# Merge-gate logits by seven half-size products in a two-layer decoder kernel; head 0's final state after the last retention step

## The chip, the cores and the metric

One NeuronCore of a Trainium2 chip runs the whole step as one launch. The metric is the device time in microseconds (us), lower is better. The program is in float32 throughout. The engines are TensorE (PE; its weight loads are listed apart as PEld), VectorE (DVE), ScalarE (ACT), GpSimd (POOL) and SyncE (SP, which issues the weight loads by DMA).

## The reference, cut to what matters

Two trunk layers of a hybrid decoder over 288 tokens: 256 of a prompt and 32 of a sample group (8 sequences of 4). Of each layer only the token-mixing half matters here:

```python
z = h @ p["w_in"][l]
u, v, q, k, vr, gr, ga, gb = jnp.split(z, ...)          # ga and gb: 1024 columns each
a = chunk_spatial_gating(gelu(u), layernorm(gelu(v)), w_s, b_s)
y, r_new = retention(rotary(q), rotary(k), vr, r0, chunk)   # 4 heads; r_new is an output
b = jax.nn.silu(gr) * head_groupnorm(y)
merged = sigmoid(ga) * (a @ w_a_out) + sigmoid(gb) * (b @ w_b_out)
x = x + gt1 * (merged @ w_o)
```

After it comes a mixture of 32 experts (16 pairs), which the change doesn't touch. `r_new` for the prompt is, for each head, one (256 x 512) matrix: the "final state" below.

## The kernel before, in words

**Weights** come from HBM as slots of 2 MB, [128, 4096] in float32, in the order in which the steps use them, into a ring of four buffers. SyncE issues the load of slot n when the last product on slot n-4 is done (`LAST_TILE`), or, where that buffer held a retention state that is written back, when the store has landed. `LOADS` gives the order.

**The order of the work** is written out by hand in `layer_steps`. Every engine walks the same list of steps and does its own part of each, in order; semaphores tie them together. PSUM has eight banks; seven of them are handed to the tiles of the steps in turn (`use`, `turn % 7`), so a tile has the bank of the tile seven places before it, and `wait_free` (L573) makes PE wait until that one has been read.

**Two ways to a product.** A direct slot (`feature_major`) multiplies 1024 inputs by 512 outputs for all 288 tokens: 4 column tiles of 8 matmuls with 288 columns. A slot by seven products (`feature_seven` for features on partitions, `token_seven` for tokens on partitions) is one Strassen-Winograd step: weights and tokens are cut in halves, and seven half-size products m1, m3, c11, m5, m6, m7, m4 take the place of eight; for features each is 2 column tiles of 4 matmuls with 144 columns. It needs four sums of the tokens (`token_sums`: s1, s3, s2, s4, made once and used by every slot with that input), four differences of weight blocks on DVE (`turn_first` L1627; `turn_rest` L1635, L1637, L1639; each 128 x 1024 elements, in place in the ring) and six additions that put the results together on DVE (`join`, L1650 to L1660). m1, m3 and c11 need no changed weights; m3 needs s4; m5, m6, m7 and m4 each wait for one more weight difference. ACT copies m1 out (`first_partial`) and applies the activation to the four quarters as they come (`bend`).

Before the change u, v (second slot), ga, a, q, k, vr, gr and b are made by seven products, and gb and the output projection o directly. gb has two slots: slot 0 is one step, ("gb", 0), and slot 1 is split into two steps of two column tiles each, ("gb", 1) and ("gc", 1).

**The stretch around the change** (layer 0 is at 280 to 428 us of the span, layer 1 runs the same steps some 774 us later):
- ("gr", 0..3), the swish-gate slots, alternate with ("st", 0..3), the sample states: PE makes eight outer products of a state, DVE adds them into the ring buffer (L2033, eight updates a state), ACT stores it back ("store").
- Then ("r1", 0), ("gb", 0), ("st", 4), ("y", 0), ("f", 0), ("fout", 0), and for the heads 1 to 3: keys transposed ("kt"), scores ("sc"), the next state ("st"), the output of the first and second chunk ("r1", "y"). For each r1 and y, DVE takes the moments (L1536, L1538) and subtracts the mean and multiplies by the gate (L2025); POOL makes the inverse root (L706, L708); ACT multiplies by it and raises `b_ready`.
- ("f", i) is the final state of head i, four matmuls into two banks; ("fout", i) copies these on ACT into a buffer and stores it. The heads in `LATE_FINAL` have theirs later, beside the router, and head 0 not.
- ("ysum", 0): the same normalisation for the samples. ("bts", 0) and ("bt", 0..7): the gated result is transposed; ACT takes bts and the even bt out of PSUM, DVE the odd ones. PE waits ahead of bts until all nine parts are normalised (`b_ready`). During ("gc", 1) DVE makes the token sums of the transposed result (`token_sums(bT, sums_b)`, L1612 to L1617), and ("b", 0..3) follow.

sgb, the sigmoid of gb, lies in the buffer `ovd`. That buffer holds the token sums for `token_seven` (`sums_t`) until the last gr slot has used them.

Of the kernel before, what the change touches and what calls it, by code (L numbers as in the profile page):

```python
# [9 lines left out]
D = 1024  # L10
# [38 lines left out]
LATE_FINAL = [(1, 2, 3), (1, 2, 3)]  # L49


def layer_steps(l):
# [14 lines left out]
    for n, step in enumerate(columns):  # L67
# [38 lines left out]
SEVEN_KINDS = ("u", "ga", "a", "q", "k", "vr", "gr")  # L106
# [9 lines left out]
BENT_AT = {s: n for n, s in enumerate((l, s) for l in range(DEPTH) for s in STEPS[l] if seven(s) and s[0] in ("v", "u", "ga", "gr"))}  # L116


def tiles_of(step, l):
# [5 lines left out]
    if step == ("gb", 1):  # L125
        return ["c0", "c1"]
    if kind == "gc":
        return ["c2", "c3"]
    if kind in ("gb", "o"):
        return ["c0", "c1", "c2", "c3"]  # L130
# [77 lines left out]
for _l in range(DEPTH):  # L208
    for _s in STEPS[_l]:
# [7 lines left out]
        elif _s in SLOT_OF and (_l, _s) not in LOADS:  # L217
            LOADS.append((_l, _s))
            if kind != "st":
                LAST_TILE[_l, _s] = (_l, ("gc", 1), "c3") if _s == ("gb", 1) else (_l, _s, tiles_of(_s, _l)[-1])  # L220
# [32 lines left out]
for _name, _width in [  # L253
    ("ident", P), ("modfold", ROWS), ("eps", 1),
    ("tri", P), ("tri_incl", P), ("tri_copies", P), ("fold", P), ("cos", TOK), ("sin", TOK),
    ("decay", 2 * HEADS * P), ("xis", 2 * HEADS * NS), ("masks", P), ("mixmask", NS),
    ("zeta", HEADS), ("zeta0", HEADS), ("zetas", NB), ("iota", PACK), ("iota4", 4), ("iota8", 8), ("iota32", NE),
# [6 lines left out]
CFIRST = P + ROWS + 1  # L264
# [17 lines left out]
def constants():  # L282
# [10 lines left out]
    put("modfold", (p[:, None] % NS == np.arange(ROWS)[None, :]))  # L293
# [26 lines left out]
    put("iota", np.broadcast_to(np.arange(PACK), (P, PACK)))  # L320
# [30 lines left out]
def build(nc, stream, consts, params, x_in, c_in, gfin, y_out, state_out, state_sample_out, v_out):  # L351
    f32, i32 = mybir.dt.float32, mybir.dt.int32
    ALU, ACT, AX = mybir.AluOpType, mybir.ActivationFunctionType, mybir.AxisListType
    with ExitStack() as ctx:
# [3 lines left out]
        def sem(name):  # L358
            return ctx.enter_context(nc.semaphore(name))
# [10 lines left out]
        modp = sb("modp", [P, 2, 512])  # L370
        ones = sb("ones", [P, P])
# [49 lines left out]
        sgb = cut(ovd[:, :], KT, TOK)  # L421
# [7 lines left out]
        kz_late = cut(prm[:, ln_at:ln_at + D], 2, 2, DK)  # L429

# [5 lines left out]
        sums_h = sums_of(work[:, SG_AT + KT * TOK:SG_AT + 2 * KT * TOK], KT // 2, RIDE)  # L436
# [1826 lines left out]
```

## Time and profile before

| | us |
|---|---|
| median of three runs | 1594.88 (1594.32 to 1595.27) |
| the profiled execution, its own time | 1594.71 |
| its span in the trace | 1592.4 |
| PE busy (share of the span) | 1554.4 (98%) |
| DVE busy | 877.7 (55%) |
| ACT busy | 270.1 (17%) |
| POOL busy | 62.8 (4%) |
| chain that ended last: PE, issue, DMA, DVE, POOL, ACT | 84%, 8%, 4%, 1%, 1%, 1% |

The time of an execution is 2.3 us more than the span of its trace. Busy is the time in which an engine has an instruction in work. Matmuls are pipelined and their ends are modelled, so a matmul's own duration is longer than the distance to the next one; costs of PE are best read as differences between starts in the timeline. One float32 matmul of the program stands as two records in the trace.

### The profile page before, as it was taken

How to read it: one execution, taken by the hardware profiler on the slowest of the kernel's cores; microseconds unless marked ns; L12 is line 12 of the kernel's file. 1: busy time of each engine (PE TensorE's matmuls, PEld its weight loads, DVE VectorE, ACT ScalarE, POOL GpSimd, SP SyncE). 2: the span in 40 equal slices, each digit the busy share in tenths (PEclk: the TensorE clock that was granted, in tenths of full speed). 3: DMA queues.
4: the chain of work that ended last, by engine and by line, in shares of the span. 5: the costliest groups of instructions: out<-in, count | busy, mean ns of one | idle time of the engine just before them, and what ended most of it. 6: DMA issues, size and time to landing. Idle time of an engine off the chain costs nothing.

```text
span 1592.4 us, 24838 instructions
## 1 busy us (share of the span) xinstructions
PE 1554.4 (98%) x9958; PEld 1070.9 (67%) x9958; DVE 877.7 (55%) x1814; ACT 270.1 (17%) x556; POOL 62.8 (4%) x107
## 2 busy tenths in 40 slices
PE   7999999999999999999999999999999998999997
PEld 3999887775797544444459998877659965444443
DVE  2776864665662634434558777556476444433436
ACT  3110000112201421111131100011130032111111
POOL 0000000001001200000000000000010011000000
PEclk9999999999999999999999999999999999999999
DMA  9824666688843799999983355548895339999993
GB/s 396 331 110 159 266 264 233 269 343 327 322 159 126 302 411 421 421 421 421 423 341 141 128 204 229 203 151 323 320 363 210 131 130 355 421 421 421 421 421 130
DMA packets 49810, 461.41 MB, mean 290 GB/s; under 512 B 5968, under 2 KB 6224, under 8 KB 10144
## 3 DMA queue, kind: packets, MB, share of 16 engines
q1 hardware_dynamic: 44656, 414.38, 65.4%
q10 hardware_dynamic: 3456, 37.75, 5.7%
q0 software_dynamic: 1584, 7.69, 1.3%
q8 instruction: 81, 1.33, 0.3%
q14 instruction: 33, 0.27, 0.0%
HBM read 415.88 MB, written 43.91 MB: 289 GB/s over the span
## 4 chain that ended last, share of the span: by engine, by line
PE 84%; issue 8%; DMA 4%; DVE 1%; POOL 1%; ACT 1%; SPq 0%; DVEq 0%; POOLq 0%; ACTq 0%
PE ps L799 84%; DMA ring<-stream 1%; DMA ovd<-sorted_rows 1%; DMA sorted_rows<-work,packed_rows 1%; POOL sorted_rows L760 0%; ACT work L1263 0%; DMA cst<-consts 0%; POOL kzm L740 0%; POOL rstd L708 0%; DVE rope L1585 0%; SPq L674 0%; DVE hT L2148 0%; POOLq L707 0%; DVEq L1529 0%; ACT hT L1263 0%
## 5 line engine op out<-in xcount | busy, mean ns | idle before, releaser
L799 PE MATMUL ps<-work,ring 128*128 128x144 f32 (+1 forms) x2624 | 358.1, 298 | 0.0
L799 PEld LDWEIGHTS ps<-work,ring 128*128 128x128 f32 x2624 | 341.0, 190 | 13.6
L799 PE MATMUL ps<-ring,work 128*64 128x512 f32 x1536 | 339.2, 595 | 2.9 <-ACT work L1263 1.3
L799 PEld LDWEIGHTS ps<-ring,work 128*64 128x64 f32 x1536 | 113.3, 137 | 211.1 <-issue 210.4
L1263 ACT ACTIVATE work<-ps 128x256 f32<-128x256 f32 (+5 forms) x228 | 97.1, 434 | 748.4 <-PE ps L799 707.5
L799 PE MATMUL ps<-ring,hT 128*32 128x128 f32 (+2 forms) x1776 | 169.9, 312 | 3.0 <-ACT hT L1263 3.0
L799 PE MATMUL ps<-hT,ring 128*128 128x144 f32 (+1 forms) x1024 | 165.6, 317 | 0.0
L799 PEld LDWEIGHTS ps<-hT,ring 128*128 128x128 f32 x1024 | 145.8, 190 | 16.6 <-issue 3.6
L799 PE MATMUL ps<-work 128*128 128x288 f32 (+3 forms) x608 | 152.1, 393 | 3.4 <-DVE hT L2122 2.6
L799 PEld LDWEIGHTS ps<-ring,hT 128*32 128x32 f32 (+1 forms) x1776 | 126.1, 132 | 39.4 <-issue 26.5
L799 PEld LDWEIGHTS ps<-work 128*128 128x128 f32 (+1 forms) x608 | 100.7, 185 | 53.9 <-issue 26.9
L799 PE MATMUL ps<-ring,ovd 128*128 128x256 f32 x576 | 130.2, 379 | 0.0
L2092 DVE TENSOR_TENSOR work<-work,ps 128x256 f32<-128x256 f32 x32 | 13.5, 421 | 208.1 <-ACT work L1263 208.1
L799 PEld LDWEIGHTS ps<-ring,ovd 128*128 128x128 f32 x576 | 109.4, 190 | 14.9
L1697 DVE TENSOR_TENSOR hT<-hT,ps 128x288 f32<-128x288 f32 x224 | 99.1, 453 | 10.8 <-PE ps L799 7.0
L2033 DVE SCALAR_TENSOR_TENSOR ring<-ring,ps 128x512 f32<-128x512 f32 x128 | 78.1, 682 | 45.3 <-PE ps L799 45.3
L1635 DVE TENSOR_TENSOR ring<-ring 128x1024 f32<-128x1024 f32 x46 | 56.4, 1225 | 58.3 <-PE ps L799 57.4
L1263 ACT ACTIVATE work<-work 128x512 f32 (+4 forms) x122 | 58.9, 525 | 150.9 <-DVE work L1657 118.7
L1627 DVE TENSOR_TENSOR ring<-ring 128x1024 f32<-128x1024 f32 x46 | 56.2, 1222 | 28.3 <-PE ps L799 27.0
L1637 DVE TENSOR_TENSOR ring<-ring 128x1024 f32<-128x1024 f32 x46 | 56.4, 1225 | 4.2
L1639 DVE TENSOR_TENSOR ring<-ring 128x1024 f32<-128x1024 f32 x46 | 56.1, 1219 | 0.0
L2128 DVE COPY work<-ps 128x512 f32<-128x512 f32 x32 | 22.1, 692 | 54.9 <-PE ps L799 54.9
(221 smaller groups left out, 1105.6 us busy)
## 6 DMA issues: line engine op xcount, KB each, us to landing
ring<-stream SPq DMA_DIRECT2D x194, 1024.0 KB, 11.0
ring<-stream SPq DMA_DIRECT2D x95, 2048.0 KB, 8.8
state_sample_out<-ring ACTq DMA_DIRECT2D x16, 2048.0 KB, 7.6
state_out<-prm ACTq DMA_DIRECT2D x8, 512.0 KB, 4.3
work<-sorted_rows SPq DMA_DIRECT2D x6, 512.0 KB, 5.3
prm<-params SPq DMA_DIRECT2D x1, 2608.5 KB, 27.3
prm<-params POOLq DMA_DIRECT2D x1, 2608.5 KB, 16.8
cst<-consts SPq DMA_DIRECT2D x1, 1651.0 KB, 20.5
```

Source lines behind the costliest of these rows:

```text
L799: return nc.tensor.matmul(out, lhsT, rhs, start=start, stop=stop, **k)
L1263: return act.activation(out, in_, func, **k)
L1627: dve.tensor_tensor(b12, b12, b11, ALU.subtract).then_inc(weights_ready, 1)
L1635: dve.tensor_tensor(b22, b22, b12, ALU.subtract).then_inc(weights_ready, 1)
L1637: dve.tensor_tensor(b11, b22, b11, ALU.subtract).then_inc(weights_ready, 1)
L1639: dve.tensor_tensor(b21, b21, b22, ALU.subtract).then_inc(weights_ready, 1)
L1697: taken(dve.tensor_tensor(hT[:, ft, :], hT[:, ft, :], out[:, 0:TOK], ALU.add), key)
L2033: taken(dve.scalar_tensor_tensor(state[:, h, dt, :], state[:, h, dt, :], math.exp(decay(h) * NT), out[:, :], ALU.mult, ALU.add), key)
L2092: taken(dve.tensor_tensor(hid[:, :, :], hid[:, :, :], up, ALU.mult), (l, pair, "gu"))
L2128: taken(dve.tensor_copy(yslot[:, 512:1024], out[:, :]), (l, pair, "y1"))
```

## The change

Both gb slots are made by `feature_seven`, in one step each. The four token sums that they need, of hT in 144-token halves, no longer exist by then (their place has been used again), so POOL makes them once more in `ovd` when the last gr slot's product m7 is done. The second gb slot moves whole to behind the transposes, and head 0's final state moves from behind ("y", 0) to ahead of the transposes. bts moves behind the bt, and each bt waits only for its own part. Since the sums fill `ovd`, the gate values move: half of them to `modp` and a new buffer `gates`, the other half to `ovd` once the sums there are used. DVE makes the token sums of bT inside ("gb", 1), between the first weight difference and the other three. A constant that nothing read (`modfold`) goes and `iota` is cut from 576 to 64 columns.

```diff
-LATE_FINAL = [(1, 2, 3), (1, 2, 3)]
+LATE_FINAL = [(0, 1, 2, 3), (0, 1, 2, 3)]
...
-        + [("r1", 0), ("store", 3), ("gb", 0), ("st", 4), ("y", 0), ("store", 4), ("f", 0), ("fout", 0), ("kt", 1), ("sc", 1), ("st", 5), ("r1", 1), ("store", 5), ("y", 1)]
-        + [("kt", 2), ("sc", 2), ("st", 6), ("r1", 2), ("store", 6), ("y", 2), ("kt", 3), ("sc", 3), ("st", 7), ("r1", 3), ("store", 7), ("y", 3)] + ([] if 3 in LATE_FINAL[l] else [("f", 3), ("fout", 3)])
-        + [("ysum", 0), ("gb", 1), ("bts", 0)] + [("bt", i) for i in range(8)]
-        + [("gc", 1)] + [("b", i) for i in range(4)]
+        + [("r1", 0), ("store", 3), ("gb", 0), ("st", 4), ("y", 0), ("store", 4), ("kt", 1), ("sc", 1), ("st", 5), ("r1", 1), ("store", 5), ("y", 1)]
+        + [("kt", 2), ("sc", 2), ("st", 6), ("r1", 2), ("store", 6), ("y", 2), ("kt", 3), ("sc", 3), ("st", 7), ("r1", 3), ("store", 7), ("y", 3)]
+        + [("ysum", 0), ("f", 0), ("fout", 0)] + [("bt", i) for i in range(8)] + [("bts", 0), ("gb", 1)] + [("b", i) for i in range(4)]
...
-SEVEN_KINDS = ("u", "ga", "a", "q", "k", "vr", "gr")
+SEVEN_KINDS = ("u", "ga", "gb", "a", "q", "k", "vr", "gr")
...
-    ("ident", P), ("modfold", ROWS), ("eps", 1),
+    ("ident", P), ("eps", 1),
...
-    ("zeta", HEADS), ("zeta0", HEADS), ("zetas", NB), ("iota", PACK), ...
+    ("zeta", HEADS), ("zeta0", HEADS), ("zetas", NB), ("iota", CAP), ...
...
+        gates = sb("gates", [P, 2, TOK])
...
-        sgb = cut(ovd[:, :], KT, TOK)
+        modp_flat = modp.rearrange("p a w -> p (a w)")
+        sgb = [cut(modp_flat[:, 0:2 * TOK], 2, TOK), gates, cut(ovd[:, 2 * TOK:4 * TOK], 2, TOK), cut(ovd[:, 0:2 * TOK], 2, TOK)]
...
+        sums_g = sums_of(ovd[:, :], KT // 2, RIDE)
...
+            if kind == "gb":
+                return [cut(rope_flat[:, 0:2 * RIDE], 2, RIDE), cut(rope_flat[:, 2 * RIDE:4 * RIDE], 2, RIDE), cut(modp_flat[:, 2 * TOK:3 * TOK], 2, RIDE)]
...
+                    elif step == ("gr", 3):
+                        s1, s4, s2, s3 = sums_g
+                        half = KT // 2
+                        a11, a12, a21, a22 = hT[:, 0:half, RIGHT], hT[:, half:KT, RIGHT], hT[:, 0:half, LEFT], hT[:, half:KT, LEFT]
+                        wait_made(pool, (l, step, "m7"))
+                        pool.tensor_tensor(s1, a21, a22, ALU.add)
+                        pool.tensor_tensor(s3, a11, a21, ALU.subtract)
+                        pool.drain()
+                        pool.tensor_tensor(s2, s1, a11, ALU.subtract)
+                        pool.drain()
+                        pool.tensor_tensor(s4, a12, s2, ALU.subtract).then_inc(gate_sums_ready, 1)
...
                 product("m1", act[:, 0:half, RIGHT], 0, 0)
-                pe.wait_ge(sums_ready, 4 * l + sums_n)
+                if step[0] == "gb":
+                    pe.wait_ge(gate_sums_ready, l + 1)
+                else:
+                    pe.wait_ge(sums_ready, 4 * l + sums_n)
                 product("m3", s4, 1, 1)
...
-                        feature_major(l, step, hT, range(4) if i == 0 else range(2))
-                    elif kind == "gc":
-                        feature_major(l, step, hT, range(2, 4))
+                        feature_seven(l, step, hT, sums_g, 0)
...
                     elif kind == "bt":
+                        tt, q = i // 4, i % 4
+                        pe.wait_ge(b_ready, l * B_DONE + 2 * q + tt + 1)
                         out = wait_free(pe, (l, step, "t"))
...
-                    elif kind == "ga":
+                    elif kind in ("ga", "gb"):
                         first_partial(l, step)
                         bend(l, step, parts_of(step), ACT.Sigmoid)
-                    elif kind in ("gb", "gc"):
-                        for name in tiles_of(step, l):
-                            out = wait_made(act, (l, step, name))
-                            taken(apply(sgb[:, 4 * i + int(name[1]), :], out[:, 0:TOK], ACT.Sigmoid), (l, step, name))
...
-                    elif kind == "gc":
-                        wait_reads(dve, [(l, ("bts", 0), "t")] + [(l, ("bt", n), "t") for n in range(8)])
-                        token_sums(bT, sums_b)
+                    elif kind == "gb":
+                        turn_first(l, step)
+                        if i == 1:
+                            wait_reads(dve, [(l, ("bts", 0), "t")] + [(l, ("bt", n), "t") for n in range(8)])
+                            token_sums(bT, sums_b)
+                        turn_rest(l, step)
+                        join(l, step, *parts_of(step)[1:])
                     elif kind == "b":
...
                         if i == 0:
-                            wait_reads(dve, tiles(l, ("gb", 0), ("c0", "c1", "c2", "c3")) + tiles(l, ("gb", 1), ("c0", "c1")) + tiles(l, ("gc", 1), ("c2", "c3")))
+                            dve.wait_ge(bent, BENT_AT[l, ("gb", 1)] + 1)
```

## Rows read from the trace of the kernel before

**Rows 1.** The page: engines over the span, and the clock by slices.
```profile
PE 1554.4 (98%) x9958; PEld 1070.9 (67%) x9958; DVE 877.7 (55%) x1814; ACT 270.1 (17%) x556; POOL 62.8 (4%) x107
PEclk9999999999999999999999999999999999999999
```

**Rows 2.** Waits of PE over the span: total, times, longest.
```profile
PE ps L799 <- ACT work L1263: 10.9, 6, 8.6
...
PE ps L799 <- ACT prm L1263: 3.0, 4, 0.9
...
PE ps L799 <- DMA ring<-stream: 1.2, 2, 1.0
```

**Rows 3.** Timeline of PE, layer 0: start, us, form, count [idle before].
```profile
348.74 1.89 PE L799 MATMUL ps<-ring,hT 128*128 128x256 f32 x8
...
355.66 15.68 PE L799 MATMUL ps<-hT,ring 128*128 128x288 f32 x64
371.27 1.07 PE L799 MATMUL ps<-ring,prm 128*32 128x512 f32 x8
...
377.23 3.60 PE L799 MATMUL ps<-work,kz 128*128 128x512 f32 x8
380.66 0.60 PE L799 MATMUL ps<-cst,work 128*128 128x128 f32 x4
```

**Rows 4.** Timeline of PE, layer 0: start of the second q slot's seven products, and what follows them.
```profile
162.13 2.23 PE L799 MATMUL ps<-hT,ring 128*128 128x144 f32 x16
...
176.05 1.92 PE L799 MATMUL ps<-ring,cT 128*32 128x512 f32 x16
```

**Rows 5.** Timeline of DVE, layer 0, around the states 4 and 5.
```profile
358.81 0.75 DVE L2025 SCALAR_TENSOR_TENSOR work<-ps,moments,work 128x512 f32<-128x512 f32 x1
373.43 4.87 DVE L2033 SCALAR_TENSOR_TENSOR ring<-ring,ps 128x512 f32<-128x512 f32 x8 [13.87 <-PE ps L799]
...
379.52 0.75 DVE L2025 SCALAR_TENSOR_TENSOR work<-ps,moments,work 128x512 f32<-128x512 f32 x1
382.61 0.42 DVE L2012 TENSOR_TENSOR scT<-ps,cst 128x256 f32<-128x256 f32 x1 [2.34 <-PE ps L799]
...
384.66 4.87 DVE L2033 SCALAR_TENSOR_TENSOR ring<-ring,ps 128x512 f32<-128x512 f32 x8 [1.43 <-PE ps L799]
```

**Rows 6.** Weight differences on DVE (page, part 5: busy, mean ns).
```profile
L1635 DVE TENSOR_TENSOR ring<-ring 128x1024 f32<-128x1024 f32 x46 | 56.4, 1225 | 58.3 <-PE ps L799 57.4
```

**Rows 7.** Weight loads beside the 144-column products (page, part 5: busy, mean ns).
```profile
L799 PEld LDWEIGHTS ps<-work,ring 128*128 128x128 f32 x2624 | 341.0, 190 | 13.6
```

**Rows 8.** Line L755, additions on POOL: ns min/median/max, first and last start us.
```profile
L755 POOL TENSOR_TENSOR work<-work x12: 790/790/794, 492.0 to 1285.6; 128x288 f32<-128x288 f32 x12
```

**Rows 9.** Timeline of PE, layer 0, from the end of ("y", 3) to the first b slot.
```profile
408.26 7.92 PE L799 MATMUL ps<-hT,ring 128*128 128x288 f32 x32
416.02 4.09 PE L799 MATMUL ps<-cst,work 128*128 128x128 f32 x36
419.95 7.93 PE L799 MATMUL ps<-hT,ring 128*128 128x288 f32 x32
427.71 86.08 PE L799 MATMUL ps<-work,ring 128*128 128x144 f32 x576
```

**Rows 10.** Timeline of ACT, layer 0: fout, then the last scalings and bts, bt.
```profile
381.10 1.07 ACT L1263 ACTIVATE prm<-ps 128x512 f32<-128x512 f32 x2
...
412.25 0.72 ACT L1263 ACTIVATE work<-work,rstd 128x512 f32<-128x512 f32 x1 [1.24 <-POOL rstd L708]
414.22 0.72 ACT L1263 ACTIVATE work<-work,rstd 128x512 f32<-128x512 f32 x1 [1.25 <-DVE work L2040]
...
416.65 1.91 ACT L1263 ACTIVATE work<-ps 128x128 f32<-128x128 f32 x6
```

**Rows 11.** Timeline of DVE, layer 0: first token sum of bT, next weight difference.
```profile
421.00 1.36 DVE L1612 TENSOR_TENSOR work<-work 128x1152 f32<-128x1152 f32 x1 [0.16 <-DVE work L2045]
...
426.41 1.22 DVE L1627 TENSOR_TENSOR ring<-ring 128x1024 f32<-128x1024 f32 x1
```

More of the change, by code:

```diff
@@ L115 @@
 SEVEN_AT = {s: n for n, s in enumerate((l, s) for l in range(DEPTH) for s in STEPS[l] if seven(s))}
-BENT_AT = {s: n for n, s in enumerate((l, s) for l in range(DEPTH) for s in STEPS[l] if seven(s) and s[0] in ("v", "u", "ga", "gr"))}
+BENT_AT = {s: n for n, s in enumerate((l, s) for l in range(DEPTH) for s in STEPS[l] if seven(s) and s[0] in ("v", "u", "ga", "gb", "gr"))}
 def tiles_of(step, l):
@@ L124, in tiles_of @@
         return ["p0", "p1", "s"]
[L125 to L129, printed above, removed]
+    if kind == "o":
         return ["c0", "c1", "c2", "c3"]
@@ L263 @@
 CW = _at
-CFIRST = P + ROWS + 1
+CFIRST = P + 1
 PFIRST = 6 * KT + 2 * KT
@@ L319, in constants @@
     put("zetas", (b[:, None] == np.arange(NB)[None, :]) * np.exp(g[h] * (NT - 1.0 - s))[:, None] * scale)
-    put("iota", np.broadcast_to(np.arange(PACK), (P, PACK)))
+    put("iota", np.broadcast_to(np.arange(CAP), (P, CAP)))
     put("iota4", np.broadcast_to(np.arange(4) - 64, (P, 4)))
@@ L429, in build, with keys_of @@
         kz_late = cut(prm[:, ln_at:ln_at + D], 2, 2, DK)
+        kz_first = cut(prm[:, ln_at + 2 * D:ln_at + 2 * D + 2 * DK], 2, DK)
+        def keys_of(i):
+            return kz_first if i == 0 else kz if i == 1 else kz_late[:, i - 2, :, :]
         def sums_of(flat, half, width):
@@ L616, in parts_of @@
                 return [merged[:, 2 * i + n:2 * i + n + 1, t] for t, n in ((RIGHT, 0), (RIGHT, 1), (LEFT, 1), (LEFT, 0))]
+            if kind == "gb":
+                return [sgb[2 * i + n][:, :, t] for t, n in ((RIGHT, 0), (RIGHT, 1), (LEFT, 1), (LEFT, 0))]
             dst = uT if kind == "u" else merged
@@ L821, in feature_major @@
             def feature_major(l, step, act, columns=range(4), merged_waits=False):
-                held = ("gb", 1) if step[0] == "gc" else step
-                w = cut(slot(l, held)[:, :], KT, 4 * P)
+                w = cut(slot(l, step)[:, :], KT, 4 * P)
                 for c in columns:
@@ L2053, in _ @@
                         if i == 0:
-                            wait_reads(dve, tiles(l, ("gb", 0), ("c0", "c1", "c2", "c3")) + tiles(l, ("gb", 1), ("c0", "c1")) + tiles(l, ("gc", 1), ("c2", "c3")))
+                            dve.wait_ge(bent, BENT_AT[l, ("gb", 1)] + 1)
                         wait_made(dve, (l, step, "c11"))
-                        taken(dve.tensor_tensor(rope[:, 0:1, RIGHT], sgb[:, f:f + 1, RIGHT], out_of(l, step, "c11"), ALU.mult), (l, step, "c11"))
+                        taken(dve.tensor_tensor(rope[:, 0:1, RIGHT], sgb[i][:, 0:1, RIGHT], out_of(l, step, "c11"), ALU.mult), (l, step, "c11"))
                         join(l, step, *sums)
                         settle()
-                        dve.tensor_tensor(rope[:, 1:2, RIGHT], sgb[:, f + 1:f + 2, RIGHT], sums[0], ALU.mult)
-                        dve.tensor_tensor(rope[:, 1:2, LEFT], sgb[:, f + 1:f + 2, LEFT], sums[1], ALU.mult)
-                        dve.tensor_tensor(rope[:, 0:1, LEFT], sgb[:, f:f + 1, LEFT], sums[2], ALU.mult)
+                        dve.tensor_tensor(rope[:, 1:2, RIGHT], sgb[i][:, 1:2, RIGHT], sums[0], ALU.mult)
+                        dve.tensor_tensor(rope[:, 1:2, LEFT], sgb[i][:, 1:2, LEFT], sums[1], ALU.mult)
+                        dve.tensor_tensor(rope[:, 0:1, LEFT], sgb[i][:, 0:1, LEFT], sums[2], ALU.mult)
                         settle()
```

11 lines of the change are left out of this document (5 added, 6 removed).

## The prediction, made before the changed kernel ran

> **What bounds the kernel now.** I read the page first. PE is busy for 98% of the span at the full clock in every slice, and no other engine for more than 55% [rows 1]. So a change pays only if it shortens PE's own work or one of PE's waits, and it costs as soon as PE waits for something new. Next the waits of PE: the largest, 8.6 of 10.9 us, is the start of the program, four of 3.0 us in total stand in the retention stretch (the key copies on ACT, two in each layer), and PE waits for a weight load only twice, 1.2 us in all [rows 2]. The weight stream is therefore no bound here, and an earlier or later slot is worth nothing by itself. After that I read the timelines of PE, DVE and ACT around the two gb slots of layer 0, to see in what order the three engines finish. Layer 1 shows the same distances, so each cost is worked out once and doubled.
>
> **gb slot 0, the product.** Direct, it takes 371.27 - 355.66 = 15.61 us of PE [rows 3]. A slot by seven products on the same input, in 144-token halves, between two steps of another form, takes 176.05 - 162.13 = 13.92 us [rows 4]. It goes from 64 records of 288 columns to 112 of 144, 124 ns from one to the next. Saved: 1.69 us a layer.
>
> One rule would turn this around. The row says that a weight load lasts 190 ns [rows 7], longer than the 124 ns between two products [rows 4], so the loads already run beside the products and beside each other. The Trainium skill, "TensorE: Matmul & The Clock Gate", section "The mechanism", says that weight loads overlap with running matmuls only where the row group differs, and these loads use all rows; by that rule a slot of 112 products would pay each load in full. By that rule, 112 times 190 ns alone would be 21 us; the trace disagrees, at 13.92 us for the whole slot. (The same page, "Step-by-step: what each phase is for", lets a load also go ahead into a background weight buffer; the trace agrees with that.)
>
> **gb slot 0, its new feeders.** (a) The sums on POOL. They may start when m7 of the last gr slot is done, at 348.74 [rows 3], and m3 needs them two products after 355.66, at 355.66 + 1.99 = 357.65 (a product is 13.92 / 7 = 1.99). That leaves 8.9 us. No row has POOL adding 576 elements; the nearest has 288 in 0.79 us [rows 8]. Bounds: four times 0.79, 3.2 us, if size cost nothing, and twice the price by elements, 12.6 us. I take the price by elements, 4 x 1.58 = 6.3 us, plus some 0.5 us of drains: done at 355.6, 2 us ahead. Cost 0, covered by m4, state 3, the first r1 and m1. Queued behind it on POOL are the key product for state 4, wanted only at about 370, and the first inverse root, which DVE calls for after 358.8 [rows 5].
> (b) The four weight differences on DVE, 1.225 us each [rows 6]. DVE is free after the first r1, at 358.81 + 0.75 = 359.56 [rows 5]. The first difference is ready at 360.8; m5, the fourth product, starts at 361.6. The others are ready at 362.2, 363.4 and 364.7, for m6, m7 and m4 at 363.6, 365.6 and 367.6. Cost 0, but the first has only 0.8 us to spare. (c) The join ends about 0.5 us after m4, at 370.1; DVE's updates of state 4 start 373.43 - 371.27 = 2.16 us after PE's start of that state [rows 3, 5], now 369.58, so at 371.7. Cost 0: DVE had stood idle 13.87 us there [rows 5]. ACT's four sigmoids fall in the same gap.
>
> **Head 0's final state.** Its four matmuls are 380.66 - 377.23 = 3.43 us of PE [rows 3], only moved. In its old place it also gave DVE time. DVE waited 2.34 + 1.43 = 3.77 us for PE between the first y and the updates of state 5 [rows 5]; with 3.43 us gone 0.34 us of that is left, so PE is just still the one that leads there. From state 5 on DVE has no idle time and everything keeps its distances, so the two short waits of PE for the key copies stay (3.0 us in both layers [rows 2]) and the end of the last y comes 1.69 + 3.43 = 5.12 us earlier. I call that moment Y; before it was 408.26 [rows 9].
>
> **The transposes.** Before, half a gb slot stood between Y and the transposes, 7.76 us, and covered ACT's last two scalings and the sum of the samples, which end at 414.22 + 0.72 = Y + 6.68 [rows 9, 10]. Now the final state alone stands there, to Y + 3.43. The nine transposes take 3.93 us, 0.437 each [rows 9]. The waits for b_ready are met in time (the last y is scaled at 412.25 + 0.72 = Y + 4.71 [rows 10]). The banks are not. bt 5 and bt 6 come seven tiles after the final state's two, which ACT copies out only behind the samples' scaling, from Y + 6.68, in 0.54 us each [rows 10]. PE has bt 0 to 4 done at Y + 5.6, begins bt 5 at Y + 7.25, bt 6 at 7.8, and bt 7, which needs bt 0's bank and so ACT's third copy, at 8.3; bts ends at Y + 9.2. Without waits it would be Y + 3.43 + 3.93 = 7.36. New wait: 1.8 us a layer. Bounds: 0, if ACT copied the final state first, and 2.5 us, if each copy brings the 0.2 us of a handover with it. I take 1.8.
>
> **gb slot 1.** Direct it is 7.76 + 7.76 = 15.52 us [rows 9]; by seven products 13.92 [rows 4]. On DVE the token sums of bT now stand between the first weight difference and the others. They need the last copy of bts: ACT is through bt 6 at Y + 9.9, and with four small copies for bts (six copies of bts and bt took 1.91 us [rows 10]) at about Y + 10.8. The sums take 426.41 - 421.00 = 5.41 us [rows 11], to Y + 16.3, and the next difference is ready at Y + 17.6. m6 is wanted at Y + 9.2 + 4 x 1.99 = 17.15. Wait: 0.45 us; the two later differences come in time. Bounds 0 and 1.5. Net: 13.92 + 0.45 - 15.52 = -1.15 us. The b slots find their sums ready, and only DVE's first b difference, behind the join, is on the way to them: at about 1.7 us after the slot's start, wanted 6 us after it.
>
> **Other edits, at 0.** The gate values in other buffers: same reads and sizes. 521 columns fewer of constants: DMA at the start, for which PE doesn't wait [rows 2]. Head 0's store moves to the transposes, where only the loads of later b slots run; the slot loads of states 6 and 7 are asked for some 2 to 5 us earlier with PE itself. The gb slot 1 is held to the end of m4 as before to the end of gc.
>
> **The sum.** A layer: -1.69 + 1.8 - 1.15 = -1.04 us; both -2.1 us. The profiled execution took 1594.71 us, so 1592.6; the median of the runs is 0.17 us above that execution, so 1592.8. Rounded for the small overlaps, **1592.7 us**, 0.14% less. What a measurement of this kernel can tell from no change is about 0.2%, 3.2 us. All that the products save is 2 x (1.69 + 1.60) = 6.6 us; two thirds of it goes back into the two waits.
>
> **Rivals.**
> (1) The waits at the transposes don't show. For it: they hang on small distances of ACT, and 0.45 us is within my rounding. Against: the order of ACT's steps is fixed and the bank count is plain. It would give 1594.9 - 6.6 = 1588.3; with only half of the waits 1590.5. Chance 0.20.
> (2) DVE leads. The slack of 0.34 us ahead of state 5 and of 0.8 us ahead of m5 are both thin. If DVE is late by 1 us at one of them and the wait for the token sums reaches its bound, a layer costs 1.5 us more: 1592.7 + 3 = 1595.7. For it: DVE takes 4.9 us of differences and six additions more in a slot. Against: 13.87 us of idle time in that place [rows 5]. Chance 0.12.
> (3) Slower: the sums on POOL come late and hold m3 of gb slot 0. It costs nothing up to 8.9 us and then its excess, twice. It ends on the slower side by more than 0.2% from (3.2 + 2.1) / 2 = 2.6 us of excess on, sums of 11.5 us; at the bound of 12.6 us it is 3.7 us a layer, 1592.7 + 7.4 = 1600.1. For it: no row shows POOL at this size, nor with inputs in four strided blocks. Against: the same operation at half the size is steady over 12 uses, 0.79 us [rows 8]. Chance 0.06.
> In (3) there is a second step. Until 359.56 every DVE instruction in that stretch reads PSUM with one operand; the weight differences read SBUF with both [rows 5, 6]. The Trainium skill, "SBUF — State Buffer", section "SBUF: two separate sides", says that a DVE instruction with two SBUF inputs and a reading GpSimd instruction exclude each other for their whole length. By that rule late sums would also push the first weight difference back; no row here shows the two side by side.
> (4) The change doesn't do what it says, or the 144-column products cost more on this buffer than on the q slot. The s4 and hT operands have the same shapes as there. Chance 0.02, 1597.
>
> **How the numbers follow.** Forecast 0.60, own range 1591.4 to 1594.3 (both waits between half and one and a half of their size). The range of 8 in 10 takes in the half of rival 1 and rival 2: 1589.9 to 1595.6. Faster by more than 0.2% means below 1591.7: rival 1 and a twelfth or so of the forecast, 0.26. Slower, above 1598.1: rival 3 and a part of 4, 0.06. The rest, 0.68, is within 0.2%.
>
> **What would show it.** In the new profile the first gb slot should last 13.9 us on PE with no wait ahead of m3 or m5; the four POOL sums some 1.6 us each; states 5 to 7 as before but 5.1 us earlier; waits of PE at bt 5, bt 6 and bt 7 of together 1.8 us, put down to ACT (the final state's copies), and about 0.5 us ahead of m6 in the second gb slot, put down to DVE; the first b slot about 1 us earlier in layer 0 and 2 us in layer 1. I am wrong if the transposes run in 3.9 us, if PE waits at m3 of gb slot 0, or if DVE's updates of state 5 start late.

## The result, and the profile after

| | before | changed |
|---|---|---|
| median of ten runs each, us | 1595.51 (1594.32 to 1596.97) | 1598.55 (1597.56 to 1600.64) |
| ratio, changed to before | | 1.0023, 95% interval 1.0015 to 1.0031 |
| span of the profiled execution, us | 1592.4 | 1597.4 |

The changed kernel is slower by 3.0 us between the medians, where 2.1 us less was forecast. That is outside the range of 8 in 10 (1589.9 to 1595.6). More than 1598.1 us had been given 0.06, and for another reason, late sums on POOL. The interval leaves "no change" out and, at 2.4 to 4.9 us, has the line of 0.2% inside it.

Every account below uses one measure: from the start of the first gb slot to the start of the b slots on PE. It holds all that the change moves apart from the constants. Before, it is 427.71 - 355.66 = 72.05 us in layer 0 [rows 3, 9] and 72.06 in layer 1. The forecast was 1.04 less in each. First the engines over the span, on the page of the changed kernel:

```profile
PE 1551.2 (97%) x10150; PEld 1080.3 (68%) x10150; DVE 908.8 (57%) x1854; ACT 271.3 (17%) x560; POOL 76.8 (5%) x115
```

Against [rows 1], PE is busy for 3.2 us less, so the products did save PE work, and yet the span is 5.0 us longer: what was gained went into waits. (Of the 5.0 us, 3.14 lie in the stretch, as counted below; 1.96 lie ahead of it, a place that varies by as much between profiles of one kernel, 0.74 between the two layers and -0.84 behind them.) These are the new ones, from the view of PE's waits over the span (total, times, longest):

```profile
PE ps L816 <- ACT work L1281: 11.9, 8, 8.7
PE ps L816 <- ACT prm L1281: 6.4, 6, 1.5
...
PE ps L816 <- ACT rope L1281: 2.2, 2, 1.1
...
PE ps L816 <- DVE ring L1649: 0.5, 1, 0.5
```

Against [rows 2], the buffer `prm` has two waits and 3.4 us more. ACT copies head 0's final state there, which makes the two new waits of 1.53 us; the other 0.35 us is a longer wait for a key copy in layer 0, taken up below. `rope` is new with two of 1.1: ACT puts product m1 of the first gb slot there. The timeline of PE in layer 0 shows where they stand (start, us, form, count, idle before and its releaser):

```profile
357.62 2.12 PE L816 MATMUL ps<-hT,ring 128*128 128x144 f32 x16
359.58 2.12 PE L816 MATMUL ps<-ovd,ring 128*128 128x144 f32 x16
362.81 2.23 PE L816 MATMUL ps<-hT,ring 128*128 128x144 f32 x16 [1.10 <-ACT rope L1281]
...
372.80 1.06 PE L816 MATMUL ps<-ring,prm 128*32 128x512 f32 x8
...
406.71 3.60 PE L816 MATMUL ps<-work,prm 128*128 128x512 f32 x8
...
414.02 1.11 PE L816 MATMUL ps<-cst,work 128*128 128x128 f32 x8 [1.53 <-ACT prm L1281]
415.58 1.94 PE L816 MATMUL ps<-cst,work 128*128 128x128 f32 x8 [0.44 <-ACT work L1281]
...
417.31 2.93 PE L816 MATMUL ps<-hT,ring 128*128 128x144 f32 x16
```

The first gb slot has its seven products in the order m1, m3, c11, m5 to m7, m4. m3 starts without a wait, so POOL's sums were in time. c11 waits 1.10 us, and the slot lasts 372.80 - 357.62 = 15.18 us in place of 13.92. The second slot's m1 lasts 2.93 us where the other products of this shape last 2.12 to 2.23: there the clock had fallen. Layer 1 has no such place, so it shows the change alone:

```profile
1134.69 2.12 PE L816 MATMUL ps<-hT,ring 128*128 128x144 f32 x16
...
1183.42 3.60 PE L816 MATMUL ps<-work,prm 128*128 128x512 f32 x8
...
1190.73 1.12 PE L816 MATMUL ps<-cst,work 128*128 128x128 f32 x8 [1.53 <-ACT prm L1281]
1192.29 1.06 PE L816 MATMUL ps<-cst,work 128*128 128x128 f32 x8 [0.44 <-ACT work L1281]
1193.19 2.13 PE L816 MATMUL ps<-hT,ring 128*128 128x144 f32 x16
...
1201.73 4.19 PE L816 MATMUL ps<-ovd,ring 128*128 128x144 f32 x32 [0.54 <-DVE ring L1649]
...
1207.72 4.45 PE L816 MATMUL ps<-work,ring 128*128 128x144 f32 x35
```

From 1134.69 to 1207.72 it is 73.03 us, 0.97 more than before. In layer 0 it is 431.84 - 357.62 = 74.22, 2.17 more. Together 3.14.

ACT tells why c11 and the transposes wait. Its timeline, layer 0, at both places (ACTq is its queue of instructions, here the issue of the store of the final state):

```profile
361.73 0.72 ACT L1281 ACTIVATE work<-work,rstd 128x512 f32<-128x512 f32 x1 [8.23 <-POOL rstd L714]
362.36 0.39 ACT L1281 ACTIVATE rope<-ps 128x288 f32<-128x288 f32 x1
...
412.67 0.72 ACT L1281 ACTIVATE work<-work,rstd 128x512 f32<-128x512 f32 x1 [1.25 <-DVE work L2054]
413.30 1.06 ACT L1281 ACTIVATE prm<-ps 128x512 f32<-128x512 f32 x2
414.45 0.34 ACTq L1290 DMA_DIRECT2D state_out<-prm  x1
414.84 2.06 ACT L1281 ACTIVATE work<-ps 128x512 f32<-128x512 f32 x4 [0.47 <-ACT prm L1281]
```

m1 was done on PE about 359.6, and ACT had been idle for 8.23 us, 2.1 of them behind the end of m1; but in ACT's order the copy of m1 stands behind the scaling of the first r1, which needs POOL's inverse root. In the second place the copies of the final state (413.30) stand behind the scaling of the samples (412.67), as predicted, and between them and the copy of bt 0 stands the issue of the store with its 0.47 us, which was not.

POOL and DVE beside the first gb slot, each in its timeline:

```profile
350.95 1.41 POOL L752 TENSOR_TENSOR ovd<-hT 128x576 f32<-128x576 f32 x1 [30.02 <-PE ps L816]
...
355.52 1.41 POOL L757 TENSOR_TENSOR ovd<-hT,ovd 128x576 f32<-128x576 f32 x1
356.89 0.61 POOL L746 TENSOR_TENSOR kzm<-kzs,cst 128x256 f32<-128x256 f32 x1
...
361.62 1.51 POOL L746 TENSOR_TENSOR kzm<-kzs,cst 128x256 f32<-128x256 f32 x1
```

```profile
361.44 1.22 DVE L1641 TENSOR_TENSOR ring<-ring 128x1024 f32<-128x1024 f32 x1
362.74 1.46 DVE L1649 TENSOR_TENSOR ring<-ring 128x1024 f32<-128x1024 f32 x1
...
382.75 4.87 DVE L2047 SCALAR_TENSOR_TENSOR ring<-ring,ps 128x512 f32<-128x512 f32 x8 [0.43 <-PE ps L816]
```

The sums end at 355.52 + 1.41 = 356.93, 2.65 us ahead of m3. The first weight difference ends at 362.66, before PE is through c11. DVE's idle time ahead of state 5 has shrunk to 0.43 us, against 1.43 [rows 5] with another 2.34 two steps earlier.

### The profile page after: what moved, and what is told of

The parts are those of the page before. It is cut to its first block, busy times and chain, and to the rows that moved or that the text cites. A ratio compares the mean times of both kernels' runs of the same rounds, so it can differ in the third digit from the quotient of the medians.

```text
span 1597.4 us, 25334 instructions
## 1 busy us (share of the span) xinstructions
PE 1551.2 (97%) x10150; PEld 1080.3 (68%) x10150; DVE 908.8 (57%) x1854; ACT 271.3 (17%) x560; POOL 76.8 (5%) x115
## 4 chain that ended last, share of the span: by engine, by line
PE 79%; issue 10%; DMA 5%; POOL 2%; DVE 2%; ACT 1%; POOLq 1%; SPq 0%; DVEq 0%; ACTq 0%
PE ps L816 79%; DMA ring<-stream 3%; DMA ovd<-sorted_rows 1%; DMA sorted_rows<-work,packed_rows 1%; ACT work L1281 1%; POOL kzm L746 0%; POOL sorted_rows L777 0%; POOL rstd L714 0%; DVEq L1543 0%; DVE rope L1599 0%; SPq L680 0%; POOLq L713 0%; DVE hT L2166 0%; POOLq L754 0%; POOLq L756 0%
## 5 line engine op out<-in xcount | busy, mean ns | idle before, releaser
L816 PE MATMUL ps<-hT,ring 128*128 128x144 f32 x960 | 129.0, 288 | 2.2 <-ACT rope L1281 2.2
L816 PEld LDWEIGHTS ps<-hT,ring 128*128 128x128 f32 x960 | 122.6, 191 | 5.4 <-issue 2.6
L1649 DVE TENSOR_TENSOR ring<-ring 128x1024 f32<-128x1024 f32 x50 | 61.7, 1235 | 54.8 <-PE ps L816 53.5
L1641 DVE TENSOR_TENSOR ring<-ring 128x1024 f32<-128x1024 f32 x50 | 61.2, 1224 | 27.4 <-PE ps L816 26.2
L1651 DVE TENSOR_TENSOR ring<-ring 128x1024 f32<-128x1024 f32 x50 | 61.3, 1225 | 4.6
L1653 DVE TENSOR_TENSOR ring<-ring 128x1024 f32<-128x1024 f32 x50 | 60.9, 1218 | 0.0
```

What stands on the lines that cost most here:

```text
L816: return nc.tensor.matmul(out, lhsT, rhs, start=start, stop=stop, **k)
L1641: dve.tensor_tensor(b12, b12, b11, ALU.subtract).then_inc(weights_ready, 1)
L1649: dve.tensor_tensor(b22, b22, b12, ALU.subtract).then_inc(weights_ready, 1)
L1651: dve.tensor_tensor(b11, b22, b11, ALU.subtract).then_inc(weights_ready, 1)
L1653: dve.tensor_tensor(b21, b21, b22, ALU.subtract).then_inc(weights_ready, 1)
```

## The experiments

The theory after the result: three places of order cost the change its gain, namely m1's copy behind the first r1's scaling, the final state's copies behind the samples' scaling, and the token sums between the weight differences. The rivals: the 144-column products themselves cost more here; the waits move and don't go; the falling clock is the main loss; the smaller constants do harm. The kernel before ran beside each group, with medians of 1594.80 us (e0 to e3), 1595.91 (e4 to e7) and 1595.21 (e8 to e10). Each ratio is the record's, with its 95% interval; it differs from the quotient of the two medians by up to 0.0008. All kernels but two do the work of the changed kernel or of before; what those two do besides is said there. "Stretch" is the measure above, as layer 0 and layer 1, and a fall of the clock is named where a profile has one.

**The changed kernel again.** No edit.

> The changed kernel once more, nothing altered. Theory A (fixed waits: c11 of the first gb slot behind a scaling on ACT, 1.1 us a layer; banks and token sums at the transposes and second gb slot, 2.5 us a layer; together 1.0 us a layer more than the products save): from the start of the first gb slot to the start of the b slots 73.0 us in both layers, 72.1 before, and 1598.5 us. Theory B (the difference is chance of the clock and of the start, where the profile showed half clock in two places): those stretches keep to 73.0 in the layers without a fall of the clock, but the falls stand elsewhere or nowhere in this profile and the time moves with them, 1596 to 1600.

Measured: 1598.61 us, ratio 1.0020 (1.0011 to 1.0029). The stretch was 74.13 and 73.00, together 3.02 more than before, again with a fall of the clock in layer 0 alone. The loss is in the stretch, and it repeats.

**m1's copy ahead of the wait for the inverse root**, on ACT:

```diff
                     elif kind in ("ga", "gb"):
-                        first_partial(l, step)
+                        if step != ("gb", 0):
+                            first_partial(l, step)
...
+                        if step == ("r1", 0):
+                            first_partial(l, ("gb", 0))
                         c = 0 if kind == "r1" else 1
                         wait_reads(act, [(l, step, f"y{c}")])
```

> ACT copies m1 of the first gb slot out before the first head's scaling, so the bank that c11 shares with m1 is free in time. Theory A: the wait of 1.1 us ahead of c11 goes in both layers with its restart, the slot lasts 13.9 us in place of 15.2, and the time falls by 2.5 us to 1596.0. Rival (the wait is moved: m5 then waits for the first weight difference, which DVE has ready 5.1 us after the slot's start, m5 is due at 5.9): the slot stays above 14.5 us and the time falls by under 1 us.

Measured: 1595.18 us, ratio 0.9999 (0.9990 to 1.0008); stretch 72.00 and 71.66, 0.45 less than before. PE's timeline, layer 0:

```profile
357.55 2.12 PE L816 MATMUL ps<-hT,ring 128*128 128x144 f32 x16
359.50 2.12 PE L816 MATMUL ps<-ovd,ring 128*128 128x144 f32 x16
361.46 2.12 PE L816 MATMUL ps<-hT,ring 128*128 128x144 f32 x16
...
371.36 1.07 PE L816 MATMUL ps<-ring,prm 128*32 128x512 f32 x8
```

c11 starts 1.96 us after m3 with no wait, and the slot lasts 371.36 - 357.55 = 13.81 us. So the products cost what [rows 4] say, and the rival that they cost more on this buffer falls. One moved copy is worth 73.03 - 71.66 = 1.37 us a layer, more than the 1.10 us shown as idle: by their starts, m3 to c11 takes 3.23 us there and 1.96 here, and c11 to m5 2.06 and 1.97.

**The final state's copies ahead of the samples' scaling**:

```diff
-        + [("ysum", 0), ("f", 0), ("fout", 0)] ...
+        + [("f", 0), ("fout", 0), ("ysum", 0)] ...
```

> ACT copies head 0's final state out ahead of the samples' scaling (step order on ACT alone; PE's order is the same). Theory A (PE waits for banks behind ACT's order): the 1.5 us ahead of bt 5 go, some 0.5 to 0.8 us stay ahead of bt 7 (bt 0's bank), the second gb slot starts 8.2 us after the last y in place of 9.8, and the time falls by about 3 us to 1595.4. Rival (ACT's work is the bound there in any order, or DVE's chain of moments): the slot starts 9.3 us or more after the last y, and the time falls by under 1 us.

Measured: 1594.22 us, ratio 0.9993 (0.9984 to 1.0001); stretch 72.05 and 71.70. PE's timeline, layer 1, from the end of the last y:

```profile
1181.47 3.60 PE L816 MATMUL ps<-work,prm 128*128 128x512 f32 x8
1184.90 3.22 PE L816 MATMUL ps<-cst,work 128*128 128x128 f32 x28
...
1189.03 1.06 PE L816 MATMUL ps<-cst,work 128*128 128x128 f32 x8 [0.91 <-ACT work L1281]
1189.93 2.13 PE L816 MATMUL ps<-hT,ring 128*128 128x144 f32 x16
```

The wait named `prm` is gone, and 8.46 us lie between the end of the last y and the second gb slot in place of 9.77. The 0.91 us left is for bt 0's bank: its copy now waits behind the samples' scaling in its turn. The wait moves and becomes smaller.

**All weight differences of the second slot ahead of the token sums**, on DVE:

```diff
-                        turn_first(l, step)
+                        turn_weights(l, step)
                         if i == 1:
                             wait_reads(dve, [(l, ("bts", 0), "t")] + [(l, ("bt", n), "t") for n in range(8)])
                             token_sums(bT, sums_b)
-                        turn_rest(l, step)
```

> In the second gb slot DVE makes all four weight differences before the token sums of the transposed result. Theory A: the 0.5 us ahead of m6 go, nothing waits for the sums at the first b slot (done 13 us after the slot's start, m3 of b wants them at 17.7), and the time falls by 1.1 us to 1597.4. Rival (the join comes later and holds the b slot's banks or its first difference): a new wait of 1 us or more in the first b slot, time 1598.5 or above.

Measured: 1597.25 us, ratio 1.0014 (1.0006 to 1.0023); stretch 72.57 and 73.89, the second with a fall. PE's timeline, layer 0, has m5 to m7 in one piece, with no wait ahead of m6:

```profile
420.60 6.04 PE L816 MATMUL ps<-ovd,ring 128*128 128x144 f32 x48
```

Layer 0, where no clock falls, is 73.38 - 72.57 = 0.81 us shorter than in e10, again more than the 0.54 us shown as idle. The slot itself lasts 13.72 us in place of 14.53.

This time the clock fell in layer 1. The same profile in stretches of 2 us (length, then busy time of PE, PEld, DVE, ACT and POOL, the granted clock, the DMA share, GB/s):

```profile
1190.00:1192.00 2.00, 2.00 (x10) 2.00 (x9) 1.78 (x2) 1.29 (x6) 0.00 (x0) 0.50 0.98 414
```

**All three together**:

> The three edits of e1 to e3 together. Theory A (the three waits are separate, each on an order that one engine keeps): first gb slot 13.9 us, last y to second gb slot 8.5 us, second gb slot 13.9 to 14.0 us; from the start of the first gb slot to the b slots 69.9 us a layer in place of 72.1 before, and 1594.8 - 4.3 = 1590.5 us, ratio 0.9973. Rival (one wait, once gone, uncovers the next: DVE's chain of states, or the sums late for the first b slot): 71 us or more a layer, ratio 0.999 or above.

Measured: 1590.53 us against 1595.91, ratio 0.9962 (0.9949 to 0.9974); stretch 69.88 and 69.52, together 4.71 less than before. PE's timeline, layer 1:

```profile
1185.59 1.06 PE L816 MATMUL ps<-cst,work 128*128 128x128 f32 x8 [0.90 <-ACT work L1281]
...
1192.37 6.04 PE L816 MATMUL ps<-ovd,ring 128*128 128x144 f32 x48
```

The three edits add up: 1.37 (e1), 1.33 (e2) and 0.81 (e3) make 3.51, and layer 1 is 73.03 - 69.52 = 3.51 us shorter than in the changed kernel. None of them touches what the change is for. The only wait of PE left in the stretch beside the two for the key copies is this 0.90. This version is faster than the kernel before by 0.3 to 0.5%.

**The waits at the transposes filled.** PE waits ahead of bt 5 until DVE has read the samples' bank, and then runs five idle matmuls on a bank that nobody reads at that time. This kernel does that much extra work.

```diff
                         pe.wait_ge(b_ready, l * B_DONE + 2 * q + tt + 1)
+                        if i == 5:
+                            wait_reads(pe, [(l, "ysample")])
+                            for _ in range(5):
+                                mm(ps[YBANK][:, P:P + SEQ], ones[:, :], xT[:, 0, 0:SEQ], True, True)
                         out = wait_free(pe, (l, step, "t"))
```

> The changed kernel with five idle matmuls of 256 columns (1.07 us) in the wait ahead of bt 5, whose results nothing reads. The wait itself stays: bt 5 starts at the same distance from the last y, 7.3 us. Theory C (the fall of the clock behind these waits costs 1.65 us where it comes, in one of two layers in most executions): no fall to half clock within 10 us of the transposes in either layer, and the time falls by 1 to 2 us to about 1597. Rival (the fall has another cause, or takes no time on the path): half clock there still in one layer, time 1598.6.

Measured: 1597.12 us, ratio 1.0007 (0.9998 to 1.0016); stretch 73.62 and 73.29. The filling costs a little itself, 0.24 and 0.26 us against e10 below, and the clock stayed up in both layers. Two details were expected otherwise: the idle matmuls take 2.23 us and not 1.07, since each is two records, and bt 5 starts 8.3 us after the last y and not 7.3. The run doesn't show that the filling keeps the clock up, since e10 below has no fall either.

**Before with the smaller constants alone** (`modfold` gone, `iota` cut):

> The kernel before with the smaller constants alone (521 columns of unread constants left out). Theory: same time as before, ratio 1.000 (0.9993 to 1.0007), though the start of the profile may show PE's wait for the second weight slot (0 to 1.5 us) and half clock behind it. Rival (the changed table shifts the transfers of the start, and its wait and fall of the clock are part of the change's price): ratio 1.001 or above.

Measured: 1595.21 us against 1595.91, ratio 0.9999 (0.9990 to 1.0008); stretch 72.04 and 72.05. The constants are no cause. It also settles a false trail. PE's view has, at the start of the changed kernel's program, a wait for a weight slot that is not in the profile of before; here it is in a kernel as fast as before (PE's timeline):

```profile
17.58 1.92 PE L798 MATMUL ps<-ring,cT 128*32 128x512 f32 x16 [1.26 <-DMA ring<-stream]
```

It varies between executions. The stretch begins at 355.65 in one profile of the changed kernel and at 357.62 in another.

**The final state back in its old place**, the rest as changed:

```diff
-        + [("r1", 0), ("store", 3), ("gb", 0), ("st", 4), ("y", 0), ("store", 4), ("kt", 1), ...
+        + [("r1", 0), ("store", 3), ("gb", 0), ("st", 4), ("y", 0), ("store", 4), ("f", 0), ("fout", 0), ("kt", 1), ...
...
-        + [("ysum", 0), ("f", 0), ("fout", 0)] ...
+        + [("ysum", 0)] ...
```

> The changed kernel with head 0's final state back behind the first y. Theory A (it cost the slack of DVE and ACT at the transposes, but it also covers 3.4 us there): PE waits at the transposes for the scaled rows instead, bt 3 for the third head's first chunk and bt 7 and bts for the last two scalings, which end 4.7 and 6.7 us after the last y; second gb slot about 7.9 us after the last y, the y itself 3.4 us later than in the changed kernel, so a layer 1.5 us longer, 1601.5 us. Rival (its own bank waits were the whole loss): the layer is shorter than 73.0 us, time below 1598.

Measured: 1601.24 us, ratio 1.0033 (1.0021 to 1.0044); stretch 75.24 and 74.86. PE's timeline, layer 1, at the transposes:

```profile
1190.30 1.97 PE L816 MATMUL ps<-cst,work 128*128 128x128 f32 x16 [1.32 <-ACT work L1281]
...
1194.81 1.06 PE L816 MATMUL ps<-cst,work 128*128 128x128 f32 x8 [2.54 <-ACT work L1281]
```

So that part of the change is worth 74.86 - 73.03 = 1.83 us a layer: without it the transposes have nothing of PE's to stand behind. The waits here are longer than any in the changed kernel, and the clock did not fall.

**POOL's sums made longer**: the second sum three times more, repeated, so that they end late. This kernel does that much extra work.

```diff
+                        for _ in range(3):
+                            pool.tensor_tensor(s3, a11, a21, ALU.subtract)
+                            pool.drain()
                         pool.tensor_tensor(s4, a12, s2, ALU.subtract).then_inc(gate_sums_ready, 1)
```

> The changed kernel with one of the four additions on POOL made three times more (its result is the same), 3 x (1.41 + 0.24) = 4.9 us ahead of the last two. The sums then end 4.9 us later, 2.3 us after m3 of the first gb slot wants them. Theory A (m3 waits for the excess, and the wait of 1.1 us ahead of c11 is then covered): m3 waits 2.3 us, c11 doesn't, the slot lasts 16.3 us in place of 15.2, and the time rises by 2.2 us, ratio 1.0035. Rival (the two waits add): slot 17.4 us, ratio 1.005. Beside it: DVE's first weight difference, with two SBUF inputs, meets the last addition of POOL; if they exclude each other, it or the addition lasts longer than 1.22 or 1.41 us, by up to 1 us.

Measured: 1602.85 us against 1595.21, ratio 1.0045 (1.0031 to 1.0059); stretch 75.69 and 75.35. PE's timeline, layer 0, first gb slot:

```profile
361.68 2.23 PE L819 MATMUL ps<-ovd,ring 128*128 128x144 f32 x16 [1.88 <-POOL ovd L760]
365.19 2.23 PE L819 MATMUL ps<-hT,ring 128*128 128x144 f32 x16 [1.29 <-ACT rope L1284]
```

and POOL's:

```profile
361.58 1.59 POOL L746 TENSOR_TENSOR kzm<-kzs,cst 128x256 f32<-128x256 f32 x1
363.14 0.18 POOL L712 TENSOR_TENSOR rstd<-moments,cst 128x1 f32<-128x1 f32 x1
```

A wait of 1.88 us at m3 does not swallow the one at c11: that is 1.29, and the two add up, to a slot of 375.19 - 357.67 = 17.52 us. The rival held, with its 17.4. Late sums push POOL's key product back, that the inverse root, that ACT's scaling, and that m1's copy. The bank is held through three engines. A part of this is not order: the key product now runs beside DVE's first weight difference (from 361.49) and lasts 1.59 us, where it is 0.61 in the changed kernel (at 356.89). Without these 0.98 us the wait at c11 would be some 0.3 us, by estimate. The meeting that was expected, of the last addition with the first difference, hardly took place: they overlap by 0.13 us and keep their lengths (1.40 and 1.22 us).

**All three, and bt 0 ahead of the samples' scaling**:

```diff
-        + [("f", 0), ("fout", 0), ("ysum", 0)] + [("bt", i) for i in range(8)] ...
+        + [("f", 0), ("fout", 0), ("bt", 0), ("ysum", 0)] + [("bt", i) for i in range(1, 8)] ...
```

> e4 with bt 0 copied out by ACT ahead of the samples' scaling (again ACT's order alone). Theory A: the 0.9 us ahead of bt 7 go; bts then waits for the samples' scaling, which ends 0.4 us later, 7.1 us after the last y; second gb slot 7.6 us after the last y in place of 8.5; 69.0 us a layer; ratio 0.9950. Rival (the sums of bT come later with bts and hold the join or the first b slot, or the wait only changes its name): 69.5 us or more a layer, ratio 0.996.

Measured: 1590.09 us, ratio 0.9960 (0.9947 to 0.9974); stretch 69.48 and 69.15, 5.48 less than before. PE's timeline, layer 0:

```profile
412.21 1.17 PE L816 MATMUL ps<-cst,work 128*128 128x128 f32 x8 [0.24 <-ACT work L1281]
```

The stretch gains 0.4 us a layer of the 0.9 of that wait. The forecast of 69.0 us was missed: the second gb slot comes 7.99 us after the last y, not 7.6, and 0.24 us of waiting is left. The runs can't tell it from the version before.

**The changed kernel a third time.** No edit.

> The changed kernel, a third profile. Theory C: half clock stands behind the transposes of one layer, as in the two profiles so far, and this stretch is 1.1 to 1.3 us longer than the other layer's. Rival (the falls have no fixed place): none, or both, or the other layer.

Measured: one run, 1596.93 us; stretch 73.38 and 73.03, and full clock in both layers. So the fall is not a fixed part of the change, and its price can be read from one kernel: 74.13 - 73.38 = 0.75 us in e0, and 74.22 - 73.38 = 0.84 in the first profile.

## Why the prediction was wrong, step by step

A layer, by layer 1 of the changed kernel, where no clock falls:

| step | predicted | measured | off |
|---|---|---|---|
| first gb slot | 13.92 | 15.18 | +1.26 |
| from the slot's end to the end of the last y (Y) | 33.56 | 1183.42 - 1134.69 - 15.18 = 33.55 | 0 |
| Y to the second gb slot | 9.2 | 1193.19 - 1183.42 = 9.77 | +0.57 |
| second gb slot | 14.37 | 1207.72 - 1193.19 = 14.53 | +0.16 |
| against before | -1.04 | +0.97 | +2.0 |

(The second row's 33.56 is the predicted Y, 408.26 - 5.12, less 355.66 and 13.92.)

**The step that failed** is gb slot 0 with its feeders. It went through POOL's sums, DVE's differences and the join, all that comes into the products, each with its slack; and all of these were in time. It did not ask who has to empty the banks. c11 takes the bank of m1, and m1 is read by ACT alone, in ACT's own order. Of ACT the prediction said in this part only that its four sigmoids fall in DVE's idle time. The trace of before has the instruction that stands ahead of m1's copy (ACT's timeline, kernel before, layer 0):

```profile
359.87 0.72 ACT L1263 ACTIVATE work<-work,rstd 128x512 f32<-128x512 f32 x1 [8.32 <-POOL rstd L708]
```

It ends 4.93 us after the slot's start at 355.66, and c11 is due after two products, at 3.98. So the wait could have been read from it. The prediction said in its part on the transposes that the banks are not met in time there, by exactly this reasoning, and did not apply it one slot earlier. e1 shows it: one copy moved on ACT, and the slot lasts 13.81 in place of 15.18. This makes 2.5 of the 4.0 us by which the two layers are off. The rivals had it nowhere either: rival 3 looked for a late feeder at m3, and 1.26 us of loss stood one product later, for another reason. Its second step, late sums that push the first weight difference back, was not seen: where late sums were forced (e8), the difference kept its 1.22 us, and what was pushed back was POOL's own queue behind the sums.

**The transposes.** The place, the name and the cause of the waits were right: 1.53 and 0.44 us where 1.8 was forecast, and e2 removes the first. The size of the whole, 9.77 for 9.2, was off by a gap on ACT that I put down to the issue of head 0's store. The prediction counted ACT's copies and said of the store only that no load is in its way; the rule that every instruction of a moved step counts would have found it. With a handover of 0.47 us ahead of the copy of bt 0, bt 7's bank comes that much later. The gap goes with the store: e9 has the same 0.47 us between its store and its copy of bt 0, and in e7, with the store elsewhere, ACT goes from the samples' scaling to bt 0's copy without one. Moving the store alone was not tried.

**m6 of the second slot.** 0.54 us of idle time for 0.45, put down to DVE; e3 removes it. The row's +0.16 hides two errors that nearly cancel: the bare slot is 13.72 us and not 13.92, and the wait costs 0.81.

One reading in rival 3 is not quite so: of DVE's instructions up to 359.56, those that finish the moments (L1538) have no operand in PSUM. Nothing hangs on it.

**Right as forecast**: the price of a slot (e1), POOL's sums hidden (four at 1.41 us, forecast 1.58), the join hidden, states 5 to 7 as before in layer 1, and head 0's final state giving back DVE's slack and no more, 0.43 us left where 0.34 was forecast.

**In layer 0 there is 0.35 us more**, 73.38 against 73.03 (e10). At state 7 PE waits 0.92 us for the key copy where it is 0.57 in layer 1, behind a gap on DVE (its timeline, changed kernel):

```profile
398.49 0.75 DVE L2039 SCALAR_TENSOR_TENSOR work<-ps,moments,work 128x512 f32<-128x512 f32 x1 [0.45 <-issue]
```

Every variant of the changed kernel has that gap in layer 0, and neither before nor e6 has it. Its cause is open.

**The sum**: 2 x 0.97 + 0.35 = 2.3 us, and with a fall of the clock in one layer 3.0 to 3.1. The medians of ten runs are 3.04 apart. That the two agree so closely is partly luck, since outside the stretch two differences of about 1 us nearly cancel, as the next part says. Rival 1, that the waits don't show, is what e4 and e9 build by hand: in the stretch they gain 4.7 and 5.5 of the 6.6 us that the products save.

**Outside the stretch two things stay open.** The first: the profiled executions of the changed kernel and its variants are longer between the two layers' stretches: 702.6 to 703.8 us, against 702.1 and 701.6 in the profiles of before and e6. In all of them but e8 PE waits for a weight load in the mixture of experts of layer 0, where before and e6 don't (PE's timeline, changed kernel):

```profile
771.73 7.09 PE L816 MATMUL ps<-ring,work 128*64 128x512 f32 x32 [0.95 <-DMA ring<-stream]
```

The second goes the other way. An execution's time is longer than its span by 1.5 to 1.6 us in every run of the changed kernel and its variants, and by medians of 2.3 to 2.6 us (1.5 to 2.9) in the runs of before and e6. So of some 1.3 us more between the layers, 0.7 to 1.0 don't show in the times. e6 has the smaller constants and is like before in both, so they are not the cause of either. Neither was tried by itself. The times follow the stretch, with these two added, to within 1.5 us; the largest misses are e4, e5 and e7, each 1.0 to 1.5 us faster than this against the kernel before that ran beside them. So a difference of 1 us between medians of separate groups of runs is not read here, and the prices of single edits are taken from the profiles.

## What to carry to other kernels

A step put in by hand has feeders and it has readers. For each tile of it, find the tile whose bank it takes, who reads that one, and what stands ahead of this read in the reader's own order; one scaling that waits for a chain of two other engines took back 1.4 of the 1.8 us that the first slot saves. When a saving doesn't show, look for such places before giving the change up: here three changes of order turned +3.0 us into -5.4 us (ratio 0.9962, 0.9949 to 0.9974), and the arithmetic was the same. A second, smaller lesson: what covered a wait before (half a slot ahead of the transposes) has a price when it is taken away (9.77 us from the last y to the second slot, where 7.36 would do), and ordering the small steps behind it wins most of that back (8.46 in e2, 7.99 in e9).

## What the runs showed of the hardware

**The clock.** The granted clock of the changed kernel in stretches of 2 us, layer 0, behind the waits at the transposes (columns as above):

```profile
414.00:416.00 2.00, 1.54 (x10) 1.28 (x11) 0.69 (x1) 1.53 (x4) 0.00 (x0) 0.88 1.04 442
416.00:418.00 2.00, 2.00 (x11) 2.00 (x10) 1.30 (x2) 1.35 (x5) 0.00 (x0) 0.50 0.99 426
```

It falls from 2.4 to 1.2 GHz when PE has already gone back to work, is 0.76 of full from 418 to 420 us and full again from 420 (1.00 from 420 to 422). It did so in layer 0 in two profiles of this kernel and in neither layer in the third, behind the same waits of 1.53 and 0.44 us. In e3 it fell in layer 1, in e7 with waits of 1.32 and 2.54 us nowhere. No other profile has one in the stretch. What decides is open. Its price depends on what follows: 0.75 and 0.84 us here, where it covers the wait ahead of m6; in e3, where nothing was left to cover, layer 1 is 1.32 us longer than layer 0, though layer 1 is otherwise the shorter by 0.35, so the price is 1.67.

**POOL beside DVE.** The same POOL instruction of 256 elements lasts 0.61 us at 356.89, beside DVE's updates of a state, which read one operand from PSUM, and 1.51 us at 361.62, beside DVE's first weight difference (361.44, 1.22 us), and the next difference lasts 1.46 in place of 1.22. The Trainium skill, "SBUF — State Buffer", section "SBUF: two separate sides", says that a DVE instruction with two SBUF inputs and a reading GpSimd instruction exclude each other; the trace agrees, in both directions. It cost nothing: in e1, where PE has no wait there, the second difference also lasts 1.46 us and the slot 13.81.
